# Two transformer layers on one NeuronCore: high-part products ahead of low-part ones at the stage openings, and Vector, Scalar and GpSimd steps reordered

## What is computed

```
h = rmsnorm(x) * (1 + scale1) + shift1
mixed = mixer(h @ w_in) ;  x = x + gate1 * rmsnorm(mixed @ w_out)
h = rmsnorm(x) * (1 + scale2) + shift2
u = h @ w_up                      # 1024 -> 2 * 2816, value and gate columns
u = conv over 3 neighbouring tokens of u, + bias
x = x + gate2 * rmsnorm((silu(gate) * value) @ w_down)
```

## Time and profile before

| | us |
|---|---|
| median of 3 runs | 1617.04 (1616.11 to 1618.12) |
| the profiled execution | 1614.98, of it the span 1613.2 |
| PE busy | 1575.6 (98% of the span), 9688 matmuls |
| DVE busy | 1279.2 (79%) |
| ACT busy | 793.4 (49%) |
| POOL busy | 381.5 (24%) |

### The profile page before, as it was taken

How to read it: one execution, slowest core, us unless ns; L and a number is a source line. 1 busy time by engine, 2 the same in 40 slices (tenths; PEclk the granted TensorE clock), 3 DMA queues, 4 the chain that set the end, 5 groups by cost and what they waited for, 6 DMA issues and landing times.

```text
span 1613.2 us, 28313 instructions
## 1 busy us (share of the span) xinstructions
PE 1575.6 (98%) x9688; PEld 1386.5 (86%) x9688; DVE 1279.2 (79%) x2255; ACT 793.4 (49%) x1483; POOL 381.5 (24%) x302
## 2 busy tenths in 40 slices
PE   8999999999999999999999999999999999999998
PEld 6788897788899999887878889967799999997886
DVE  7876587867999999966668556988689999998575
ACT  6432235638655565533373323274665565563333
POOL 0031043001455555200000400700035455541000
PEclk9999999999999999999999999999999999999999
DMA  9343265351222222454414414736313222235451
GB/s 369 131 131 97 87 224 174 85 165 53 66 86 83 82 87 85 149 157 157 150 40 144 137 53 137 261 100 153 72 43 100 78 91 78 91 91 171 129 183 66
DMA packets 65494, 195.04 MB, mean 121 GB/s; under 512 B 15361, under 2 KB 16769, under 8 KB 65153
## 3 DMA queue, kind: packets, MB, share of 16 engines
q1 hardware_dynamic: 50114, 175.54, 35.2%
q10 hardware_dynamic: 15296, 18.39, 3.5%
HBM read 187.05 MB, written 6.85 MB: 120 GB/s over the span
## 4 chain that ended last, share of the span: by engine, by line
PE 77%; DVE 12%; issue 3%; ACT 3%; DMA 2%; ACTq 1%; DVEq 0%; SPq 0%
PE bank L2083 13%; PE bank L2084 13%; PE bank L2085 13%; PE bank L2550 9%; PE bank L2552 9%; PE bank L2551 9%; DMA raw<-in_stream 2%; DVE w_lo L1940 1%; DVE w_lo L1353 1%; PE bank L2363 1%; PE bank L2350 1%; PE bank L2105 1%; PE bank L2423 1%; PE bank L2247 1%; DVE ada_sq L1364 1%
## 5 line engine op out<-in xcount | busy, mean ns | idle before, releaser
L777 ACT ACTIVATE w_hi<-raw 128x1024 fp32r<-128x1024 f32 (+1 forms) x120 | 123.2, 1029 | 394.0 <-PE bank L2085 329.9
L1353 DVE TENSOR_TENSOR w_lo<-raw,w_hi 128x1024 fp32r<-128x1024 f32 (+1 forms) x128 | 156.9, 1231 | 166.9 <-ACT w_hi L777 166.6
L2083 PE MATMUL bank<-w_hi,aT_lo 128*128 128x512 f32 x560 | 226.3, 404 | 2.3 <-DVE aT_lo L1786 2.0
L2084 PE MATMUL bank<-w_lo,aT_hi 128*128 128x512 f32 x560 | 221.3, 395 | 0.0
L2085 PE MATMUL bank<-w_hi,aT_hi 128*128 128x512 f32 x560 | 220.9, 394 | 0.0
L2550 PE MATMUL bank<-aT_hi,w_lo 128*128 128x322 f32 x640 | 199.3, 311 | 7.8 <-DVE u L1951 4.6
L2551 PE MATMUL bank<-aT_lo,w_hi 128*128 128x322 f32 x640 | 198.7, 311 | 0.0
L2552 PE MATMUL bank<-aT_hi,w_hi 128*128 128x322 f32 x640 | 198.1, 310 | 0.0
L1251 ACT ACTIVATE w_hi<-raw 128x512 fp32r<-128x512 f32 x200 | 117.8, 627 | 93.2 <-POOL raw L660 93.2
L2083 PE MATMUL bank<-w_hi,m_lo 128*128 128x512 f32 x400 | 158.8, 397 | 2.9 <-DVE m_lo L1985 2.6
L2084 PE MATMUL bank<-w_lo,m_hi 128*128 128x512 f32 x400 | 157.3, 393 | 0.0
(11 more groups left out here) (275 smaller groups left out, 3817.1 us busy)
## 6 DMA issues: line engine op xcount, KB each, us to landing
raw<-in_stream SPq DMA_DIRECT2D x304, 512.0 KB, 3.6
lead<-in_lead SPq DMA_DIRECT2D x16, 512.0 KB, 10.5
bias<-in_bias ACTq DMA_DIRECT2D x8, 896.0 KB, 10.8
na_v<-vn ACTq DMA_DIRECT2D x2, 1280.0 KB, 5.7
x<-in_xs SPq DMA_DIRECT2D x4, 512.0 KB, 12.4
vt<-na_v ACTq DMA_DIRECT2D x16, 128.0 KB
gb_mix<-gates ACTq DMA_DIRECT2D x2, 1024.0 KB, 5.0
gb_ffn<-gates ACTq DMA_DIRECT2D x8, 256.0 KB, 4.5
```

The costliest lines, as they stand in the source:

```text
L777: act.activation(w_hi[:, g % 4, 0:n], raw[:, s % 4, 0:n], ACT.Copy).then_inc(hi_done, 1)
L1353: dve.tensor_tensor(w_lo[:, g % 4, 0:n], raw[:, s % 4, 0:n], w_hi[:, g % 4, 0:n].bitcast(F32), ALU.subtract).then_inc(raw_free[s % 4], 1)
L2083: pe.matmul(out, ll, rh, start=start, stop=False)
L2084: pe.matmul(out, lh, rl, start=False, stop=False)
```

## The change

The same instructions, in another order, with one wait more on POOL and the wait for a low part split from the wait for its high part on PE. In `turn_mix` (not shown) `stats` and `weight` of ACT and `root`, `weight` of DVE change places in the same way as in `turn_ffn`.

```diff
@@ POOL, before the loop
                 pool.wait_ge(s_lo_done, at(s_lo_done, layer, 3))
+                pool.wait_ge(blk_lo, at(blk_lo, layer, 5))
                 pool.tensor_tensor(s_sum[:, 0], h_part(0, 1), s_sum[:, 1], ALU.subtract)...
@@ ACT turn_ffn
                 squares(1)
+                mod_(0)
                 stats(1)
                 scale(1)
-                mod_(0)
                 squares(2)
                 hi(0)
                 mod_(1)
-                weight(0)
                 stats(2)
                 scale(2)
                 hi(1)
+                weight(0)
@@ ACT, before the loop
-                gate_silu(None, 1)
                 for n in range(2, 6):
                     block_high(n, 1, 1)
+                gate_silu(None, 1)
@@ DVE turn_ffn
                 mod_(0)
+                post_tile(0, 2, layer)
                 mod_(1)
-                post_tile(0, 2, layer)
+                root(2)
                 low(1, 0, layer)
-                root(2)
+                low(1, 1, layer)
+                mod_(2)
                 weight(0)
-                mod_(2)
-                low(1, 1, layer)
                 low(1, 2, layer)
@@ DVE, the loop
                         column_conv(i, e, 1)
+                        first_with_sixth(*after(i, e))
                         block_low(6, *after(i, e))
+                        with_seventh(*after(i, e))
                         block_low(1, i + 1, e)
-                        block_low(0, i + 1, e)
-                        first_with_sixth(*after(i, e))
-                        with_seventh(*after(i, e))
                         gate_late(*after(i, e))
                         gate_sum(*after(i, e))
+                        block_low(0, i + 1, e)
                         value_early(*after(i, e))
                         for n in range(2, 5):
                             block_low(n, i + 1, e)
@@ DVE, after the loop
                 column_conv(last, 1, 0)
-                split_lo(W_DOWN0 + 2, layer)
                 column_conv(last, 1, 1)
                 for kt in (2, 3):
                     down_low(0, kt, m_lo[:, kt, :], m_hi[:, kt, :])
+                split_lo(W_DOWN0 + 2, layer)
@@ PE
+            def high_pass(tt, q):
+                out, tok = bank[in_bank(0, tt)][:], toks(tt)
+                for kk in range(2):
+                    k, col = 2 * q + kk, slice(kk * W, (kk + 1) * W)
+                    pe.matmul(out, aT_hi[:, k, tok], w_hi[:, q, col], start=k == 0, stop=False)
+                    pe.matmul(out, aT_hi[:, k, tok], w_lo[:, q, col], start=False, stop=False)
...
             def lead_block(h, tt):
-                pe.wait_ge(norm_lo, NT * h + tt + 1)
+                pe.wait_ge(norm_hi, NT * h + tt + 1)
                 for q in (2 * h, 2 * h + 1):
                     if tt == 0:
                         pe.wait_ge(*freed(stream_of(q), 0))
+                    high_pass(tt, q)
+                pe.wait_ge(norm_lo, NT * h + tt + 1)
+                for q in (2 * h, 2 * h + 1):
+                    i_ = low_pass(tt, q)
...
+            def first_block(tt, layer):
+                pe.wait_ge(norm_hi, at(norm_hi, layer, tt + 1))
+                for q in range(2):
+                    ...
+                    high_pass(tt, q)
+                if tt < 2:
+                    norm_transposes(0, tt + 1, layer)
+                pe.wait_ge(norm_lo, at(norm_lo, layer, tt + 1))
+                for q in range(2):
+                    i_ = low_pass(tt, q)
...
+            def up_opening(layer):
+                pe.wait_ge(hi_done, at(hi_done, layer, W_UP0 + 1))
+                pe.wait_ge(norm_hi, at(norm_hi, layer, NT + 3))
+                ...  8 matmuls w_hi * aT_hi
+                pe.wait_ge(raw_free[0], at(raw_free[0], layer, S_UP0 // 4 + 1))
+                ...  8 matmuls w_lo * aT_hi
+                pe.wait_ge(norm_lo, at(norm_lo, layer, NT + 3))
+                ...  8 matmuls w_hi * aT_lo
```

More of the change, by code:

```diff
@@ L1014, in turn_mix @@
                 scale(1)
-                stats(2)
                 weight(2)
                 weight(3)
+                stats(2)
                 mod_(1)
+                hi(1)
                 scale(2)
-                hi(1)
                 squares(3)
@@ L1026, in turn_mix @@
                 scale(3)
-                stats(4)
                 mod_(3)
                 hi(3)
+                stats(4)
                 scale(4)
@@ L1705, in turn_mix @@
                 lo(0)
+                weight(2)
+                weight(3)
                 root(2)
                 mod_(1)
-                weight(2)
-                weight(3)
                 lo(1)
@@ L1715, in turn_mix @@
                 post_tile(1, 4, layer)
-                root(4)
                 mod_(3)
                 lo(3)
+                root(4)
                 mod_(4)
@@ L2128, in lead_transposes, with low_pass @@
                 i_.then_inc(norm_tp, 1)
+            def high_pass(tt, q):
[4 more added lines that the diff above has]
+                    pe.matmul(out, aT_hi[:, k, tok], w_lo[:, q, col], start=False, stop=False)
+            def low_pass(tt, q):
+                for kk in range(2):
+                    k = 2 * q + kk
+                    i_ = pe.matmul(bank[in_bank(0, tt)][:], aT_lo[:, k, toks(tt)], w_hi[:, q, kk * W:(kk + 1) * W],
+                                   start=False, stop=k == KD - 1)
+                return i_
             def lead_block(h, tt):
-                pe.wait_ge(norm_lo, NT * h + tt + 1)
+                pe.wait_ge(norm_hi, NT * h + tt + 1)
                 for q in (2 * h, 2 * h + 1):
@@ L2144, in lead_block @@
                     i_.then_inc(in_done, 1)
-            def first_block(tt, qs, layer):
-                pe.wait_ge(norm_lo, at(norm_lo, layer, tt + 1))
-                for q in qs:
+            def first_block(tt, layer):
+                pe.wait_ge(norm_hi, at(norm_hi, layer, tt + 1))
+                for q in range(2):
                     if tt == 0:
                         pe.wait_ge(*freed(stream_of(q), layer))
[L2152 to L2156, removed]
+                    high_pass(tt, q)
[4 more added lines that the diff above has]
+                    i_ = low_pass(tt, q)
                     if tt == NT - 1:
                         i_.then_inc(w_used, 1)
-                if tt < NT - 1 and qs[-1] == 3:
+                if 2 <= tt and tt + 1 < NT:
+                    norm_transposes(0, tt + 1, layer)
+                for q in range(2, 4):
+                    if tt == 0:
+                        pe.wait_ge(*freed(stream_of(q), layer))
+                    high_pass(tt, q)
+                    i_ = low_pass(tt, q)
+                    if tt == NT - 1:
+                        i_.then_inc(w_used, 1)
+                if tt < NT - 1:
                     i_.then_inc(in_done, 1)
@@ L2429, in up_product @@
                     i_.then_inc(w_used, 1)
+            def up_opening(layer):
+                out, tok = bank[0][:, 0:N0], slice(0, N0)
+                pe.wait_ge(hi_done, at(hi_done, layer, W_UP0 + 1))
+                pe.wait_ge(norm_hi, at(norm_hi, layer, NT + 3))
+                for k in range(KD):
+                    pe.matmul(out, w_hi[:, 0, k * P:(k + 1) * P], aT_hi[:, k, tok], start=k == 0, stop=False)
+                pe.wait_ge(raw_free[0], at(raw_free[0], layer, S_UP0 // 4 + 1))
+                for k in range(KD):
+                    pe.matmul(out, w_lo[:, 0, k * P:(k + 1) * P], aT_hi[:, k, tok], start=False, stop=False)
+                pe.wait_ge(norm_lo, at(norm_lo, layer, NT + 3))
+                for k in range(KD):
+                    pe.matmul(out, w_hi[:, 0, k * P:(k + 1) * P], aT_lo[:, k, tok], start=False, stop=k == KD - 1)
             pe.wait_ge(ones_done, 1)
@@ L2533, in _ @@
                         second_half(tt, (q,), layer)
-                for c in range(4):
+                up_opening(layer)
+                for c in range(1, 4):
                     pe.wait_ge(raw_free[c], at(raw_free[c], layer, S_UP0 // 4 + 1))
-                    pe.wait_ge(norm_lo, at(norm_lo, layer, NT + 3))
                     for k in range(KD):
@@ L2632, in _ @@
                     for tt in range(NT):
[L2633 to L2638, removed]
+                        first_block(tt, layer + 1)
 def bind(nc, arrays, outs):
```

## The result

| | before | after |
|---|---|---|
| median | 1617.58 us (4 runs) | 1659.26 us (4 runs, 1656.45 to 1662.92) |
| the profiled execution | 1614.98, span 1613.2 | 1662.92, span 1661.1 |
| PE busy | 1575.6 us | 1599.0 us |

The ratio is 1.0258, 95% interval 1.0235 to 1.0282: the change makes the kernel 2.6% slower. The forecast was 1650 in a range of 1630 to 1662.

What follows compares the result with a forecast made beforehand. PE bounds the kernel, busy 1575.6 of 1613.2 us at full granted clock. A layer +22.9 - 3.2 - 2.4 + 0 = +17.3, both +34.6, turn between -1.8: +32.8 on 1614.98 is 1647.8, plus 2.06 for the median: 1650, range 1630 to 1662.

Steps and rivals of the forecast that it cites:

- The loop, +22.9 a layer: Feed-forward loop: 17 halves a layer, each 1.35 us longer, +22.9 us a layer (17.0 to 27.2).
- The chain: In each loop half: DVE's block 0 releases POOL's third_sum, then ACT's high part, then DVE's block 2; 2.81 or 2.62 us.
- the period: Time of one loop half, between successive gate_sum starts: from 12.35 us to 13.7.
- the second meeting: In the loop, POOL's fourth_sum still runs when DVE's block 2 may start; block 2 ends 0.27 to 0.48 us late.
- the 45 foretold: Inside the loop, PE waiting for DVE's gate_sum (L1966) about 1.3 us a half, in all near 45 us.
- firm bound on what a reorder can win: Whole kernel: no reorder can win more than the 37.6 us in which PE is idle.
- The entry, -3.2 a layer: Entry of the feed-forward loop: waits for w_lo and u go, gate_sum comes late; net -3.2 us a layer (0 to -4.4).
- The turn to the feed-forward, -2.4: Stage opening, twice: PE's waits of 1.0 for xn and 1.3 for the low part go; -2.4 us a layer (0 to -2.6).
- The exit, 0: Behind the loop: another stretched chain pass costs about 1.0 us, split_lo(2) behind down_low gives 1.0 back; 0 (-1.0 to +1.2).
- The turn between the layers, -1.8: Once: high pass fills two 1.0 us waits for xn and one of 0.2, then 0.5 for hi(1); -1.8 (0 to -2.3).
- The start, 0: Kernel start, once: 2.0 us of low-part waits go, weight low-part waits cost 0.5 at both halves; 0 (-1.0 to +0.5).
- The rival with no gains at the turns: Nothing gained at the turns adds 13 us: 1663 us; chance 0.05.

Runs made afterwards that it cites:

- experiment 2: The kernel before with one edit: DVE's order inside the feed-forward loop is that of after. 1666.17 us, ratio 1.0300 to before.
- experiment 3: The kernel after with block 0 two places earlier in DVE's loop order, ahead of gate_late and gate_sum. 1626.6 us, ratio 1.0061 to before.
- experiment 5: The kernel after with POOL's fourth_sum cut to 64 of 512 columns. 1643.21 us, ratio 1.0176 to before.
- experiment 6: Experiment 1 without the wait that the change put on POOL before the loop. 1612.51 us, ratio 0.9976 to before.
- experiment 8: The kernel before with lead_block of after alone. 1617.84 us, ratio 1.0007 to before.
- experiment 9: The kernel after with lead_block and DVE's loop order of before, but first_with_sixth ahead of the blocks in the loop's first half, written out. 1607.06 us, ratio 0.9943.
- experiment 10: Experiment 9 with m_lo of the third and fourth granule ahead of the conditioning sum and weight split behind the loop. 1605.65 us, ratio 0.9925 to before.
- experiment 1: The kernel after with DVE's order inside the feed-forward loop put back to that of before. 1611.13 us, ratio 0.9961 to before.
- experiment 4: The kernel after with block 0 three places earlier in DVE's loop order and lead_block of before. 1610.22 us, ratio 0.9960 to before.
- experiment 7: The kernel after with lead_block of before. 1658.04 us, ratio 1.0249 to before.

## Why the prediction was right, term by term

- **The loop, +22.9 a layer.** Measured +23.2 and +24.9. The chain (2.82 us for 2.81), the period (13.71 for 13.7) and the second meeting (0.47 and 0.27 for 0.48 and 0.27) came out as worked out, and experiments 2, 3 and 5 show each by itself. PE's rows show 36.0 us of waits for DVE's two steps, not the 45 foretold: the matmul rows cover much of the rest. For the same reason PE's idle time is no firm bound on what a reorder can win, as the prediction has it: the busy time itself went from 1575.6 to 1599.0 us with the same matmuls. In layer 1 a half is 0.1 longer in every version in which DVE sets the pace (12.50, 12.89, 13.82). The rows of after place it in front of the first convolution step, where DVE waits 0.81 us for ACT in layer 1 and 0.70 in layer 0 (means); why is open.
- **The entry, -3.2 a layer.** Right in size: -1.1 ahead of the first `gate_sum` and -2.2 behind it. One part had the wrong cause: I gave the wait for ACT's `u` and its restart (1.0) to POOL's wait and wrote that nothing behind `gate_silu` was late. Without POOL's wait that gain stays (experiment 6: 17.46 us between the first two, before 18.45), so it is not POOL's; ACT's moved `gate_silu` is what is left, and it was not tried alone.
- **The turn to the feed-forward, -2.4.** Measured -3.0 and -3.3, less the 1.1 of POOL's wait: -1.9 and -2.2 (experiment 6, without that wait: 89.8 us for 91.7, -1.9). `xn` was as foretold. The 1.3 for the low part went too, but a product of 256 columns 20 us later now waits 0.7 for its own low part (L2449 <- L1404).
- **The exit, 0.** This is the step that failed. "One more pass through the stretched chain costs about 1.0" is +2.3 and +2.4. In layer 0 block 2 starts 3.04 us after the loop's last `gate_sum`, before 1.25: 0.60 of the 1.79 is block 0 itself, which now stands behind `gate_sum`, the rest the wait for the chain (1.53, where DVE waited 0.35 for PE). Another 0.64 comes since the three blocks of that half meet `fourth_sum` and then `gated`, which runs right behind it there: 3.52 us for the three, 2.88 before, when they met `gated` alone. And `split_lo(2)` behind `down_low`, which was to give back the wait of 1.0, gives nothing: from the last `gate_sum` to the end it takes 164.8 us in both kernels. PE's wait for `m_lo` has only moved, from 11.4 to 18.7 us behind the last `gate_sum`. Its own wait of 2.46 us for that `gate_sum` and the slower clock after it cost nothing further (last section).
- **The turn between the layers, -1.8.** The three waits went, 2.2 in all, and a new one of 1.0 for the weight's low part (L1354) came, not foreseen: about -1.0.
- **The start, 0.** Right (experiment 8), though the profile of after alone seemed to say 6.6.

The forecast was 9 us low: the exit 4.7, the loop 2.3, the turn between the layers about 1, the turns to the feed-forward and the entries 0.4 together; the rest can't be told from the spread. The rival with no gains at the turns (1663) is nearer to 1659.3 than the forecast is, but by its number only: the gains came to about -11.5 of the -13 forecast, and what was missing is the exit.

## What to carry to other kernels

Where an engine's order holds two ends of a chain that runs through others, count what stands between the ends, in time: each instruction taken from there beyond the slack returns as a wait in every turn of the loop (0.95 us moved, 0.94 us waited). Gains at a stage's entry are paid once, a loop's loss 17 times, so take the entry's order for the first pass alone, as experiments 9 and 10 do. And compare a stretch in several executions before giving a few us of it to the code.

## What the runs showed of the hardware

**The profile's clock column doesn't show the start.** It reads 1.00 in every slice up to 260 us in both kernels, while the matmuls of the start run at the 1.2 GHz distance (0.43 us for 512 columns); only the distances of the rows tell. So "at full granted clock" in the prediction is not so for the first 28 us of before.

**A wait of PE can be followed by a slower clock, and not each time.** Granted clock and DMA are the last columns; in front of them busy us of PE, PEld, DVE, ACT, POOL in each stretch, after:

```profile
480.00:500.00 20.00, 19.28 (x130) 18.90 (x129) 15.38 (x29) 10.99 (x21) 9.45 (x8) 1.00 0.19 56
680.00:700.00 20.00, 17.27 (x81) 14.84 (x80) 19.20 (x32) 12.55 (x18) 6.74 (x2) 0.91 0.48 144
```

And PE behind that wait:

```profile
686.71 0.39 PE L2590 MATMUL bank<-aT_hi,w_lo 128*128 128x322 f32 x1 [2.46 <-DVE u L1966]
686.93 0.31 PE L2591 MATMUL bank<-aT_lo,w_hi 128*128 128x322 f32 x1
...
688.43 0.47 PE L2590 MATMUL bank<-aT_hi,w_lo 128*128 128x322 f32 x1
688.70 0.47 PE L2591 MATMUL bank<-aT_lo,w_hi 128*128 128x322 f32 x1
```

Starts 0.15 apart at first, then 0.27 (1.2 GHz) until 691 us: about 1.7 us of PE's work lost. Over ten profiles there are 20 waits of PE of 1.8 to 2.5 us, at the loop's entry or behind the loop, and nine were followed by this: six of eight behind the loop, three of twelve at the entry, with the same code too (experiment 1: layer 0 yes, layer 1 no). Behind the six of 1.4 to 1.8 us in experiments 3 and 4 there was none. What decides it stays open.

What it costs depends on who sets the pace afterwards. At the entry of a loop in time PE does: the periods of 12.44 for 12.35 are 17 x 0.09 = 1.5 us. Behind the loop DVE does, and nothing is lost. PE's next wait for `m_lo` ends 18.7 us after the last `gate_sum` with the slower clock (after, layer 0) and without it (experiment 7, layer 1); PE only waits less there:

```profile
704.67 0.47 PE L2084 MATMUL bank<-w_hi,m_lo 128*128 128x512 f32 x1 [0.43 <-DVE m_lo L1986]
```
```profile
1508.48 0.47 PE L2084 MATMUL bank<-w_hi,m_lo 128*128 128x512 f32 x1 [1.33 <-DVE m_lo L1986]
```

From the last `gate_sum` (685.95 and 1489.76) that is 18.72 in both, and from there to the end it takes 164.8 us in layer 1 of every version except the last.

**POOL's length hangs on DVE.** The same `s_sum` took 3.05 us beside DVE's blocks and 2.75 behind them (experiment 6), and `gated` 1.6 us in the loop and 5.5 (695.36 to 700.83 us after) beside DVE's weight splits behind it. By these rows both sides of a meeting pay, and the rows of POOL alone don't tell that it waited. No edit tested the second of them by itself.
